# A hybrid convolution, RWKV-7 and mixture-of-experts layer: the vector engine's row numbers lose their wait for an earlier scatter

## The reference, cut to what matters

```
scores = sigmoid(t @ w_router)                  # 512 x 64
idx    = top 8 of the experts in the 4 best groups
gate   = scores[idx] / sum(scores[idx]) * 2.5
for each expert e, for its tokens xb:
    y = (silu(xb @ we_gate[e]) * (xb @ we_up[e])) @ we_down[e]
routed = sum over a token's 8 experts of gate * y
x      = x + gt2 * rmsnorm(routed + shared)
```

## Time and profile before

| what | value |
|---|---|
| median of three runs | 1566.86 us (1565.52 to 1571.6) |
| profiled execution, its own time | 1567.21 us |
| its span | 1565.4 us |
| mean granted clock of TensorE | 0.934 |
| PE matmul, busy | 1375.4 us, 88% |
| VectorE, busy | 1034.0 us, 66% |
| ScalarE, busy | 613.6 us, 39% |
| POOL, busy | 399.4 us, 26% |
| DMA, mean rate | 218 GB/s |

### The profile page before, as it was taken

The page is one execution under the profiler, slowest core; times in us unless marked ns, Lnnn a source line. Parts: engine busy times, 40 slices in busy tenths (PEclk is TensorE's granted clock), DMA queues, the critical chain, the costliest instruction groups (busy, mean ns, idle before and its releaser), DMA issues. The chain is left out here.

```text
span 1565.4 us, 18873 instructions
## 1 busy us (share of the span) xinstructions
PE 1375.4 (88%) x5795; PEld 931.8 (60%) x5795; DVE 1034.0 (66%) x1646; ACT 613.6 (39%) x928; POOL 399.4 (26%) x350
## 2 busy tenths in 40 slices
PE   6899999866598999597999999999999999999947
PEld 3677677525498344354666666666666666666613
DVE  4459999778733433236777777777777776877607
ACT  3322131251124202203555555555555555555501
POOL 0334344321000000001233333333333333332200
PEclk9899998876799999688999999999999999999969
DMA  8343534100000800670688888888899888888448
GB/s 310 123 162 137 185 127 169 68 0 1 1 1 0 322 1 27 224 321 16 236 338 324 316 333 339 314 346 309 343 364 354 313 326 322 330 323 296 157 187 356
DMA packets 85841, 341.35 MB, mean 218 GB/s; under 512 B 16982, under 2 KB 20240, under 8 KB 58660
## 3 DMA queue, kind: packets, MB, share of 16 engines
q1 hardware_dynamic: 65976, 307.07, 51.5%
q0 software_dynamic: 19584, 33.60, 5.8%
q10 hardware_dynamic: 236, 0.09, 0.0%
HBM read 334.40 MB, written 44.04 MB: 242 GB/s over the span
## 5 line engine op out<-in xcount | busy, mean ns | idle before, releaser
L2116 PE MATMUL py<-down_ring,hT 128*128 128x512 f32 x544 | 251.7, 606 | 1.1 <-ACT hT L2054 0.9
L2077 PE MATMUL p_gate_up<-gate_up_high,x_hi 128*128 128x512 f32 x544 | 230.3, 423 | 23.9 <-DVE x_lo L2153 23.3
L2144 DVE TENSOR_TENSOR gate_up_low<-gate_up,gate_up_high 128x1024 fp32r<-128x1024 f32 x204 | 244.1, 1218 | 7.1 <-ACT gate_up_high L2035 6.9
L2077 PE MATMUL p_gate_up<-gate_up_high,x_lo 128*128 128x512 f32 x544 | 216.5, 398 | 0.0
L2077 PE MATMUL p_gate_up<-gate_up_low,x_hi 128*128 128x512 f32 x544 | 216.4, 398 | 0.0
L2006 POOL TENSOR_TENSOR carrier<-offsets 1x1 f32<-1x1 f32 x136 | 71.3, 525 | 547.4 <-DVE tokens L2162 384.4
L2035 ACT ACTIVATE gate_up_high<-gate_up 128x1024 fp32r<-128x1024 f32 x204 | 203.9, 1051 | 1.0 <-issue 0.8
L2116 PEld LDWEIGHTS py<-down_ring,hT 128*128 128x128 f32 x544 | 98.5, 191 | 100.7 <-issue 100.2
L2077 PEld LDWEIGHTS p_gate_up<-gate_up_high,x_hi 128*128 128x128 f32 x544 | 103.8, 191 | 86.5 <-issue 61.6
L269 POOL TENSOR_TENSOR ring_lo<-ring,w_hi 128x2048 fp32r<-128x2048 f32 x19 | 94.6, 4980 | 173.0 <-ACT w_hi L310 173.0
L429 PE MATMUL pz<-h_hi,w_hi 128*128 128x512 f32 x304 | 123.3, 405 | 6.7 <-DVE h_lo L497 3.6
(11 more groups left out here) (363 smaller groups left out, 2119.6 us busy)
## 6 DMA issues: line engine op xcount, KB each, us to landing
down_ring<-in_we_down SPq DMA_DIRECT2D x68, 1024.0 KB, 5.5
gate_up<-in_we_gate SPq DMA_DIRECT2D x51, 1024.0 KB
gate_up<-in_we_up SPq DMA_DIRECT2D x51, 1024.0 KB
ring<-in_w_ada SPq DMA_DIRECT2D x12, 2048.0 KB, 8.0
ring<-in_w_in SPq DMA_DIRECT2D x9, 2048.0 KB, 9.2
x_again<-in_we_gate SPq DMA_DIRECT2D x17, 1024.0 KB
x_again<-in_we_up SPq DMA_DIRECT2D x17, 1024.0 KB
rows<-expert_rows SPq DMA_DIRECT2D x6, 2048.0 KB, 18.5
```

What stands on the lines that cost most here:

```text
L2077: mm = pe.matmul(pgu[u % 2][:, :], x[:, u % 2, k, :], weights, start=(k == 0 and n == 0), stop=(k == KD - 1 and n == 2))
L2116: mm = pe.matmul(py[half][:, :], hT[:, u % 2, k, :], weights[:, k, half * N:half * N + N], start=(k == 0), stop=(k == 1))
L2144: V.tensor_tensor(moe.low[u % RING][:, :, piece(i), :], moe.gate_up[u % RING][:, :, piece(i), :], exact(w_hi[:, u % 2, :, piece(i), :]), A ...
```

## The change

In VectorE's row_numbers the call of `left` is taken out. Nothing else is changed: VectorE computes the row numbers of a block as soon as its token numbers are there, and y_half, which follows it in the list, still waits for the scatter two blocks back of its own block.

More of the change, by code:

```diff
@@ L2165, in row_numbers @@
                 dve.wait_ge(s_num, b + 1)
-                left(dve, b, u)
                 V.tensor_tensor(row_ids[:, u % 4, :], number[:, u % 4, 2:3], moe.offsets[:, 1:2], ALU.add).then_inc(s_rows, 1)
```

## The result

The changed kernel took 1506.61 us (median of four runs, 1505.56 to 1509.81) against 1566.64 us before: ratio 0.9614, 95% interval 0.9589 to 0.9639. It is faster, by 60.0 us in the medians. The profiled execution took 1509.81 us, with a span of 1508.0, that is 57.4 us less than the span of before.

A forecast was written before the change was run, and what follows sets the result against it. PE was taken as the bound, held by VectorE's wait in a loop with one scatter in flight. 51.2 us above the 10.33 us floor less 2.1 gave 49.1; 1567.2 - 49.1 = 1518.1 us, forecast 1518, range 1512 to 1535.

The forecast's parts named there:

- The floor: Expert stage, case A: without the wait every step takes 10.33 us, giving 1518 us, own range 1515 to 1524; chance 0.72.
- the one free step of before: Step near 760 us, no scatter out yet: taken as a sample of the changed kernel, px 10.33 us apart.
- the spacing of px: Starts of x's transposes on PE, once a step: 65 steps in 722.65 us, 51.2 us above the floor.
- the idle gaps: PE's gaps in the steady expert stage, the other count of its loss: 34.1 us, giving 1533 us.
- The sum over the stage: Saving in the expert stage's 65 steps: 51.2 us above the floor less 2.1, 49.1 us.
- part 3: The 14.50 us step where the loops change: half of its 4.17 us above the floor stays, 2.1 us.
- the late steps: Four steps after 1435 us, where POOL waits for each scatter before its next gather: up to 1 us each may stay.
- The loop: One scatter in flight between VectorE's row_ids and POOL: 2.11 plus 8.19 us, 10.30 together, or 13.05 with the first scatter.
- B: Expert stage: another wait of VectorE holds PE just above the floor; 34.1 us gained, 1533 us; chance 0.13.
- E: Expert stage, halfway: one step in four stays held, keeping a quarter of the 49 us; 1530 us; chance 0.06.
- C: VectorE's y_half inherits the stall through its same kind of wait, nothing or almost nothing gained; 1567 us; chance 0.05.
- D: DMA engines: the lull behind the weight loads closes, PE waits for gathered rows, slower; 1585 us; chance 0.04.

The follow-up runs named there:

- the 23 later runs: Further runs of the unchanged kernel before: median 1562.88 us; ratio of the changed kernel in this wider comparison 0.9659.
- the wait on y: Changed kernel, but VectorE's y waits for the scatter one block back instead of two: 1558.61 us, ratio 0.9979 to the kernel before.
- the wait three back: Kernel before, but its row numbers wait for the scatter three blocks before their own block: 1507.26 us, ratio 0.9659.
- the exchange: Kernel before with POOL issuing a step's scatter ahead of the gather instead of behind it: 1554.26 us, ratio 0.9934.
- the row numbers behind y: Kernel before with row_numbers and y_half exchanged in VectorE's list, wait for the scatter one block back kept: 1550.79 us, ratio 0.9934.
- light down loads: Kernel before with down weights loaded only in part from the fifth block on, 0.25 of 1 MB: 1520.53 us, ratio 0.9731.

## Why the prediction was wrong, point by point

**The floor** held: 10.33 us a step was read off two steps and the one free step of before, and 60 steps now take a mean of 10.324. The view that gave it, the spacing of px, was right against the idle gaps, which would have said 1533 us.

**The sum over the stage** said 49.1 us and measured 50.8. Of the missing 1.7 us, 1.3 are in part 3: the step where the loops change was left 2.1 us above the floor, split by halves without a row for it, and is 0.8 us above it. Of the 4.17 us over the floor there in the kernel before, PE's 2.07 us of idle time and the clock of 0.88 over the step (0.12 of 14.5 us is 1.7) make up 3.8, and both went with the change. Another 0.4 us is the floor, taken as 10.33 for 10.324, and the late steps, allowed up to 1 us each, took 10.15 to 10.47.

**What failed** is the sentence "The sum goes against the profiled execution, 1567.2 us" together with "That execution is 0.3 us above the median of the three runs, so I forecast 1518 for both": it took the other 845 us of the kernel as equal in both, a term put at nothing without a reason. They are not: 6.6 us of the difference between the two profiles lie ahead of the stage, where the granted clock differed, and some 9 of that between the medians (60.0 less 50.8) lie outside the stage; that these too are the clock's is inferred, since no profile shows those runs. The three runs shown, within some 6 us of each other, hid a spread that the 23 later runs show as 1552.76 to 1573.53 us. The 7.8 us that the prediction itself gave a measurement, taken off the lower end of 1512, would have made it 1504, with the result inside.

**The loop**: its consequence was right and its mechanism half right. That the wait for the scatter one block back was the cause, the kernels with the wait on y and with the wait three back show. But its parts "2.11 us from row_ids to the scatter's issue, 8.19 us from there to the next row_ids" are no fixed times that add up. An earlier issue bought 13.5 us only; the release keeps its place in PE's step, and the two things that moved it were the gather issued ahead of the scatter and the bytes of the weight loads. Nor do the steps of before all lie between 10.30 and 13.05 us: four take 13.23, 13.46, 13.56 and 14.50.

**Rivals.** B and E (another wait holds PE, or one step in four stays held) did not come: PE has one wait of 0.5 us in 664. C (y inherits the stall) was excluded as said: y waited for PE alone. D (the lull closes) did not come: PE never waited for gathered rows, and the DMA engines carried 349 GB/s, near the 344 foretold. But the order of gather and scatter that it rested on does matter, here for the scatter, and it acted in the kernel before as well, whose fixed loop gained 10.4 us by the exchange. What would show each step right (waits of 0.4, 0.9 and 0.5 us, scatter about 4 us before px, clock 1.00) came as listed.

## What to carry to other kernels

When an engine waits for a transfer, ask first how many transfers old the one it names must be; a wait that names one block too young costs whatever goes beyond the engine's room in a step, here 1.8 us, even on an engine that is idle a quarter of the time. Its total says little: from 760 to 1400 us it was 114.2 us with the row numbers behind y and 113.0 with light down loads, and the stages of these two were 37 and 10 us over that of the changed kernel. Issue order within a queue can count as much as issue time: with the row numbers behind y, exchanging two entries of POOL's list brought the fixed loop to the same 10.33 us as removing the wait did. And before a range is given for a whole kernel, take the spread of the parts that the change doesn't touch into it; a stage measured from landmark to landmark repeats to 0.2 us where the whole moves by 20.

## What was not expected of the hardware

A scatter of 60 rows on average (4096 over 68 blocks) took a median of 8.4 to 11.4 us from issue to release, depending on the kernel, and issuing it 2.3 us earlier made it 2.5 us longer. With the clock's dips ahead of the expert stage, the same unchanged code ended up to 15.9 us apart between executions (first px at 722.38 and at 738.30). And POOL was busy 197.63 us in 664 where it had been busy 251.00 in 724, with the same instructions: among them the tiny addition ahead of a scatter, 0.94 us in the kernel before in 57 steps, while VectorE's gate_up_low ran, took 0.18 us in nearly all steps of the changed kernel, where it fell outside that operation; its cause was not tried.
